# Four more value slots in the attention stage's page ring, and values two groups of pages later

## The reference

```python
kp = cache_k[i, page_table].reshape(db, past_len, MOBA_HEADS, HEAD_DIM)
vp = cache_v[i, page_table].reshape(db, past_len, MOBA_HEADS, HEAD_DIM)
...
k_mean = jnp.mean(kb.astype(jnp.float32), axis=3)
gate = jnp.einsum('bhtd,bhnd->bhtn', qh.astype(jnp.float32), k_mean)
_, sel = lax.top_k(gate, n_sel)        # the 3 best blocks of 256 tokens, and the own block
logits = q . k * scale - slope * distance, masked to the chosen blocks
p = softmax(logits);  out = p @ v
```

## Time and profile before

| | before |
|---|---|
| median of the runs | 1219.59 us (1218.74 to 1225.41) |
| profiled execution | 1221.69 us, its span 1220.0 us |
| PE busy | 1101.5 us, 90% of the span |
| DVE busy | 694.1 us, 57% |
| ACT busy | 562.6 us, 46% |
| POOL busy | 289.2 us, 24% |
| DMA | 182.58 MB, mean 150 GB/s |
| key page loads (kring) | 128 of 256 KB, median 3.7 us from issue to landing |
| value page loads (vring) | 128 of 256 KB, median 4.2 us from issue to landing |

### The profile page before, as it was taken

One profiled execution on the slowest core, in us unless ns is written; L12 is line 12 of the kernel. 1 busy time (PEld: TensorE's weight loads), 2 busy tenths in 40 slices (PEclk: granted clock), 3 DMA queues, 4 the chain that ended last, 5 costly groups with the idle time before them and its releaser, 6 DMA issues.

```text
span 1220.0 us, 20034 instructions
## 1 busy us (share of the span) xinstructions
PE 1101.5 (90%) x7015; PEld 990.8 (81%) x7015; DVE 694.1 (57%) x1191; ACT 562.6 (46%) x886; POOL 289.2 (24%) x274
## 2 busy tenths in 40 slices
PE   5999879976889999897999999988999699999995
PEld 3999768845555666566999999978999699999993
DVE  4753644454777777645666663445564666665333
ACT  3337501244666666645544443445333744543424
POOL 8400113320466667613100000213003300000101
PEclk9989958969899999988999999998999899999997
DMA  7334200064789889662444543443435244553411
GB/s 218 114 136 144 69 1 1 1 203 142 252 291 297 292 295 306 194 204 69 138 138 148 166 167 122 130 139 116 159 138 147 70 138 139 162 167 135 145 53 43
DMA packets 119121, 182.58 MB, mean 150 GB/s; under 512 B 6128, under 2 KB 59471, under 8 KB 118990
## 3 DMA queue, kind: packets, MB, share of 16 engines
q1 hardware_dynamic: 116274, 173.30, 43.2%
q0 software_dynamic: 2784, 8.47, 2.4%
HBM read 176.12 MB, written 5.63 MB: 149 GB/s over the span
## 4 chain that ended last, share of the span: by engine, by line
PE 73%; DVE 9%; ACT 7%; issue 3%; DMA 3%; POOL 2%; SPq 2%; DVEq 0%; ACTq 0%; POOLq 0%
PE bank L1652 68%; PE bank L1946 3%; DMA kring<-cache_k 2%; ACT hi L709 2%; POOL xl L652 1%; ACT xres L993 1%; DVE xres L1108 1%; DVE kTl L1108 1%; DVE lo L1101 1%; SPq L426 1%; POOL lo L625 1%; PE bank L1662 1%; ACT xh L709 1%; DMA xtok<-x_sample 1%; ACT kTh L709 0%
## 5 line engine op out<-in xcount | busy, mean ns | idle before, releaser
L1652 PE MATMUL bank<-xh,hi 128*128 128x320 f32 x1184 | 372.3, 314 | 33.5 <-POOL xl L652 26.1
L1652 PE MATMUL bank<-xl,hi 128*128 128x320 f32 x1184 | 370.1, 313 | 0.0
L1652 PE MATMUL bank<-xh,lo 128*128 128x320 f32 x1184 | 369.6, 312 | 0.0
L1101 DVE TENSOR_TENSOR lo<-raw,hi 128x2048 fp32r<-128x2048 f32 x102 | 242.2, 2375 | 188.6 <-ACT hi L709 188.6
L1652 PEld LDWEIGHTS bank<-xh,hi 128*128 128x128 f32 x1184 | 226.1, 191 | 36.2 <-issue 31.3
L709 ACT ACTIVATE hi<-raw 128x2048 fp32r (+1 forms) x102 | 194.8, 1910 | 107.6 <-PE bank L1652 107.6
L1652 PEld LDWEIGHTS bank<-xl,hi 128*128 128x128 f32 x1184 | 226.3, 191 | 0.1
L1652 PEld LDWEIGHTS bank<-xh,lo 128*128 128x128 f32 x1184 | 226.0, 191 | 0.0
L1108 DVE TENSOR_TENSOR kTl<-bank,kTh 128x512 fp32r<-128x512 f32 x128 | 88.0, 689 | 77.3 <-ACT kTh L709 75.8
L1652 PE MATMUL bank<-hh,hi 128*128 128x320 f32 x416 | 129.4, 311 | 1.3 <-DVE hraw L1108 1.3
L1652 PE MATMUL bank<-hh,lo 128*128 128x320 f32 x416 | 128.5, 309 | 0.0
(11 more groups left out here) (387 smaller groups left out, 1498.4 us busy)
## 6 DMA issues: line engine op xcount, KB each, us to landing
raw<-w_up SPq DMA_DIRECT2D x44, 1024.0 KB
kring<-cache_k SPq DMA_DIRECT2D x128, 256.0 KB, 3.7
vring<-cache_v SPq DMA_DIRECT2D x128, 256.0 KB, 4.2
raw<-w_down SPq DMA_DIRECT2D x8, 2048.0 KB
raw<-w_in_mix SPq DMA_DIRECT2D x7, 2048.0 KB
raw<-w_in_sc SPq DMA_DIRECT2D x8, 1024.0 KB
raw<-w_down SPq DMA_DIRECT2D x4, 1536.0 KB
raw<-w_out_mix SPq DMA_DIRECT2D x2, 2048.0 KB
```

Source lines behind the costliest of these rows:

```text
L1101: dve.tensor_tensor(lo[:, p], weight(n)[:, :, 256 * p:256 * p + 256], hi[:, p], ALU.subtract)\
L1652: return pe.matmul(out, lhsT, rhs, start=start, stop=stop, **kw)
```

## The change

The value pages get four more slots, in the half of `raw` that is idle during attention, so eight in all; the keys keep their two. The list of places is now the same for all readers (`kpages`, `vpages`, with `KS` = 2 and `VS` = 8). A value pair waits for POOL's work on the pair eight before it instead of four. Beside that, SP's step `n` issues pairs 2n - 12 and 2n - 11 instead of 2n - 10 and 2n - 9: values stand six groups behind keys instead of five. The units at which ACT, POOL and PE use the pairs are unchanged. The first value load also waits for the state's stores (7 stores), since the state lies in the same half of `raw`, and the load of slot `S_OUT + 1` into that half waits until all values are split. `load_list` of steps 0 and 1 moves ahead of two waits on PE and DVE.

```diff
-params_in xtok_in hist_in wba_in pt_in raw_in k_in0 k_in1 v_in0 v_in1 v_in2 v_in3 s0_in0 stores
+params_in xtok_in hist_in wba_in pt_in raw_in k_in0 k_in1 v_in0 v_in1 v_in2 v_in3 v_in4 v_in5 v_in6 v_in7 s0_in0 stores
...
+        spare_raw = raw[:, 0:4096].rearrange("p (j c) -> p j c", c=512)
+        kpages = [kring[:, 1], kring[:, 0]]
+        vpages = [vring[:, i] for i in range(4)] + [spare_raw[:, 2 * i:2 * i + 2] for i in range(4)]
+        KS, VS = len(kpages), len(vpages)
+        V_LAG = 12
...
-            for n in range(4 * NB + 5):
+            for n in range(4 * NB + V_LAG // 2):
+                if n < 4 * NB:
+                    load_list(n)
                 if n == 0:
                     PE.wait(sp_, "o1")
                     DV.wait(sp_, "qg2")
                 if n == 1:
                     PE.wait(sp_, "stS2")
                 if n < 4 * NB:
-                    load_list(n)
-                    after(sp_, "kT_mm", 4 * n - 4)
-                    x = (n + 1) % 2
-                    load_pair(kring[:, x, 0:2], a["cache_k"][0], f"k_in{x}", 2 * n)
-                    load_pair(kring[:, x, 2:4], a["cache_k"][0], f"k_in{x}", 2 * n + 1)
-                if n == 5:
+                    after(sp_, "kT_mm", 4 * (n - KS) + 4)
+                    k = kpages[n % KS]
+                    load_pair(k[:, 0:2], a["cache_k"][0], f"k_in{n % KS}", 2 * n)
+                    load_pair(k[:, 2:4], a["cache_k"][0], f"k_in{n % KS}", 2 * n + 1)
+                if n == V_LAG // 2:
                     PE.wait(sp_, "po1")
-                for m in (2 * n - 10, 2 * n - 9):
+                    sp_.wait_ge(s["stores"], 16 * 7)
+                for m in (2 * n - V_LAG, 2 * n - V_LAG + 1):
                     if m >= 0:
-                        after(sp_, "v_lo", m - 3)
-                        load_pair(vring[:, m % 4], a["cache_v"][0], f"v_in{m % 4}", m)
+                        after(sp_, "v_lo", m - VS + 1)
+                        load_pair(vpages[m % VS], a["cache_v"][0], f"v_in{m % VS}", m)
                         listed.pop(2 * m), listed.pop(2 * m + 1)
             sp_.wait_ge(s["stores"], 16 * 11)
+            sp_.wait_ge(s["v_lo"], VALL)
             slot_free(S_OUT + 1)
...
-                act.wait_ge(s[f"v_in{n % 4}"], 32 * (n // 4 + 1))
+                act.wait_ge(s[f"v_in{n % VS}"], 32 * (n // VS + 1))
...
-                copy(vhs[n % 3], vring[:, n % 4]).then_inc(s["v_hi"], 1)
+                copy(vhs[n % 3], vpages[n % VS]).then_inc(s["v_hi"], 1)
```

More of the change, by code:

```diff
@@ L624, in _ @@
                 pool.wait_ge(s["v_hi"], n + 1)
-                pool.tensor_tensor(vls[n % 3], vring[:, n % 4], vhs[n % 3], ALU.subtract).then_inc(s["v_lo"], 1)
+                pool.tensor_tensor(vls[n % 3], vpages[n % VS], vhs[n % 3], ALU.subtract).then_inc(s["v_lo"], 1)
                 b = n // VUNITS + 2
@@ L1466, in v_lo @@
                 dve.wait_ge(s["v_hi"], n + 1)
-                tt(vls[n % 3], vring[:, n % 4], vhs[n % 3], ALU.subtract).then_inc(s["v_lo"], 1)
+                tt(vls[n % 3], vpages[n % VS], vhs[n % 3], ALU.subtract).then_inc(s["v_lo"], 1)
             kT_lo(0)
@@ L1940, in transpose @@
                 g, h = divmod(n, H)
-                x = (g + 1) % 2
                 if h == 0:
-                    pe.wait_ge(s[f"k_in{x}"], 64 * (g // 2 + 1))
+                    pe.wait_ge(s[f"k_in{g % KS}"], 64 * (g // KS + 1))
                 after(pe, "kT_lo", n - 2)
                 for j in range(4):
-                    ins = pe.transpose(bank[n % 3][:, P * j:P * j + P], kring[:, x, j, P * h:P * h + P], ident[:, :])
+                    ins = pe.transpose(bank[n % 3][:, P * j:P * j + P], kpages[g % KS][:, j, P * h:P * h + P], ident[:, :])
                 ins.then_inc(s["kT_mm"], 1)
```

## The result

| | before | after |
|---|---|---|
| median of the runs | 1221.12 us (4 runs, 1218.74 to 1225.41) | 1233.83 us (4 runs, 1231.56 to 1238.18) |
| ratio, with its 95% interval | | 1.011 (1.0082 to 1.0138) |
| profiled execution, its span | 1221.69 us, 1220.0 us | 1232.57 us, 1230.8 us |
| key page loads, median to landing | 3.7 us | 3.6 us |
| value page loads, median to landing | 4.2 us | 4.9 us (`vring`), 4.8 us (`raw`) |

The change costs 12.7 us, 1.1%, where +5.4 was forecast; 1233.8 lies just outside the range of 1213 to 1233. The forecast was added to 1219.6 us, and the same kernel measured 1221.1 beside the changed one, so 1.5 us of the level are the base; what has to be explained is 12.7 against 5.4. The granted clock of TensorE was the same over the span (0.949 before, 0.950 after), and so is the work. What changed is what the engines wait for.

What follows compares the result with a forecast made beforehand. The attention stage was taken to hang on the order of waits, with DVE's run covering PE's key stalls. Pair 6's delays, 3 x 1.2 + 3 x 0.6 = +5.4 us, on 1219.6 gave 1225.0 us; range 1213 to 1233.

Steps and rivals of the forecast that it cites:

- The bound: Attention rounds: PE's work, then the DVE and ACT chain set the 28.4 us; key stalls lie in the chain's shadow.
- rival A: Attention: key stalls are on the path, so all 13.0 us of key waits come back, 1206.6 us; chance 0.13.
- One sign that the prediction named: PE's wait before a round's first value matmul was to grow from 1.0 to 2 us or more.
- Eight slots: Key loads: SP never waits for the subtraction, keys 21 go out 2.0 us sooner; gain at unit 2 none.
- rival B: Pairs land by E + 6.2, DVE's run is not pushed; 1.9 us come back at unit 14, 1217.7 us; chance 0.20.
- Pair 6 at unit 0: ACT waits 2.5 us for pair 6, pushing DVE's run 1.2 us in three rounds, 0.6 in three: +5.4 us.
- Pair 0, "hidden, by 0.4 us": ACT before the exponentials: pair 0 lets them start at 431.6, the DVE run pushes them to 431.96 anyway; no cost.
- Pairs 2 and 4, "none, up to 1 us a round": ACT at units 8 and 12: up to 2 us late, no cost, up to 1 us a round if landings are slower.
- Start, end and last weight load: Stage's ends: later first values cost nothing; last weight load between nothing and +1.9 us, taken as nothing.
- Rival C: Bursts overlap, each landing grows by 1 us: 1231.0 us, or 1232.9 with the last weight load late; chance 0.25.
- Slower: Whole kernel: a measured time above 1225.7 us, made up of C and the rest of the forecast's own case; chance 0.36.

Runs made afterwards that it cites:

- e1: Eight value slots with the old lag of five groups (V_LAG 10 instead of 12 in the changed kernel): 1218.85 us beside 1218.47, ratio 1.000.
- e9: Block sums and ranks, some 1.84 us of DVE's work per round, left out of the kernel with eight slots and the old lag: 1207.48 us beside 1219.36, 0.9893.
- e7: The changed kernel with pairs 6 and 7 of each sequence issued one group earlier, as before the change: 1230.88 us beside 1219.36, 1.0092.
- e12: The changed kernel with pairs 0, 1, 6 and 7 issued one step earlier, only pairs 2 to 5 late: 1225.09 us beside 1220.46, 1.0030.
- e3: The kernel before, with only the stage's last weight load held until all values are split: 1217.65 us beside 1218.47, 0.9999.
- e10: The changed kernel with the odd value pairs' loads left out, their readers taking the even pair's page: 1230.38 us beside 1220.46, 1.0070.
- e8: Block sums and ranks, some 1.84 us of DVE's work per round, left out of the kernel before: 1212.68 us beside 1219.36, 0.9934.
- e6: The changed kernel with pairs 0 and 1 of each sequence issued one group earlier, as before the change: 1231.9 us beside 1219.36, 1.0087.

## Why the prediction was wrong

**The bound.** Right. DVE's run covers the key stalls: e1 removes them for nothing, e9 shows that they are worth 5 us where the run is shorter. The faster rival A is out. One sign that the prediction named did not come: PE's wait before the first value matmul was to grow from 1.0 to 2 us or more. It is 1.03 us in the kernel after, and also in e1, where the keys come in time; so it was not the measure of PE's slack. What PE has over shows earlier in the round, where it waits for a unit's rest on DVE:

```profile
469.52 0.47 PE L1660 MATMUL bank<-kTh,qp 128*128 128x512 f32 x1 [0.78 <-DVE kTl L1116]
```

**Eight slots.** Right: no gain at unit 2, and 1.7 us in the trace of e1 at unit 14, where 1.9 had been worked out under rival B.

The loads hang on two points of a round: E, the end of unit 13's transposes, releases pair 6's burst, and the end of unit 1's transposes, which I call E1, releases pair 0's. In the round shown these are 451.40 and 458.60:

```profile
450.80 0.60 PE L1953 MATMUL bank<-ident,kring 128*128 128x128 f32 x4
...
458.00 0.60 PE L1953 MATMUL bank<-ident,kring 128*128 128x128 f32 x4
```

The six full rounds after, against what the prediction had:

| us | forecast | measured, mean (range) |
|---|---|---|
| pair 6 starts on ACT, from E | 7.4 | 7.76 (7.18 to 8.33) |
| unit 3's rest starts, from E | 9.1 | 9.33 (8.75 to 9.90) |
| shift ends, from E | 15.6 | 15.81 (15.23 to 16.38) |
| E1, from E | 6.17 | 7.03 (6.18 to 7.76) |
| pair 0 starts on ACT, from E1 | 7.4 | 8.10 (7.56 to 8.51) |
| exponentials start, from E | 15.6 | 16.58 (16.04 to 17.15) |

**Pair 6 at unit 0.** The mechanism was as described; a size was off. Unit 3's rest starts 1.58 us behind the start of pair 6's rounding in each of the six rounds, and the way from E to it grew by 6.8 us in the sum, where 5.4 had been worked out. (The +5.0 of the first table is another thing: it counts from the biases, which the late pairs 2 and 4 had moved already.) The term that was mis-sized is the 7.15 us from the first key issue to the pair, which took 7.58 for pair 6. Over the 18 pairs, the pair's second DMA left SP 2.71 us after the first key issue on the mean (2.45 forecast) and landed 5.00 us later (4.7).

**Pair 0, "hidden, by 0.4 us".** This step failed: +4.4 us. The cover of 0.4 is the difference of two paths, DVE's run behind pair 6 and ACT's copy of pair 0. A landing that is longer for both moves both and leaves the cover. What moved pair 0's path alone is its start: the text left E1 where it had been, 422.52 - 416.35 = 6.17 us behind E, and it came 7.03 behind E, in the round shown 7.20. And pair 0's landing took 0.3 us more than pair 6's (7.92 from the first key issue). So pair 0 let the exponentials start at E + 16.6, when the shift had been ready since E + 15.8. The margin was also smaller than the spread of the landings that I had read (4.4 to 5.5 in one burst), so "hidden" was not a value to take.

**Pairs 2 and 4, "none, up to 1 us a round".** This step failed as well, and it is what moved E1. Two units of slack between ACT and PE for the pair itself were counted, but not what is queued behind `v_hi` on ACT. With pair 4 at 452.71 two key copies and the queries' rounding wait behind it, DVE stands for 3.35 us, and unit 2's rest moves by 0.6 us:

```profile
454.29 1.30 DVE L1116 TENSOR_TENSOR kTl<-bank,kTh 128x512 fp32r<-128x512 f32 x2 [3.35 <-ACT kTh L717]
```

PE shows the same wait twice, before a product of unit 15 and one of unit 0, both ahead of unit 1's transposes:

```profile
455.13 0.41 PE L1660 MATMUL bank<-kTl,qp 128*64 128x512 f32 x1 [0.28 <-DVE kTl L1116]
...
456.50 0.49 PE L1660 MATMUL bank<-kTh,qp 128*128 128x512 f32 x1 [0.29 <-POOL qp L619]
```

In e1, where no pair is late, E1 comes 6.2 us behind E in every round; in e7, where pair 6 is early and pair 4 late, 6.4 to 7.3 us. So it is not pair 6 that moves it. The delay of the biases itself costs nothing here, since unit 3's rest waits for pair 6 anyway; it comes out in e12, where pair 6 is in time. In round 2 the late values reach into PE's own part: ACT waits 3.05 us for pair 2 (at 322.48), PE behind it for DVE's rests, and E comes 8.99 us after the first value matmul instead of 7.18.

It is the argument that the prediction made for pair 6, and did not make for pair 4. Together: the forecast was 5.4, the rounds grew by 12.9; of the 7.5 between them 4.4 are pair 0, 1.8 are E in round 2, and 1.4 (6.8 - 5.4) the later landing of pair 6, up to 0.1. This is read from one trace and from what e1, e7 and e12 change in it; a run with pairs 2 to 5 alone in time was not made.

**Start, end and last weight load.** Right: nothing (e3, and no difference behind the six rounds).

**The rivals.** Rival C had the direction: landings are later. Its price, 1 us for each of six landings, gave 1231.0. The landings grew by 0.6 on the mean, of which e10 puts 0.4 on the odd pairs' traffic; its reason, that a burst lies over the next, is not shown (see e10). The loss was larger all the same: C laid it on pair 6 alone, where pairs 4 and 0 pay too. B is out: pair 6 came 7.2 to 8.3 us behind E, and B needed 6.2. The rule of the Trainium skill (DMA: Bandwidth & Descriptors, on where the fixed cost goes in the anatomy of one DMA) gives, as an estimate, 5.6 us from the first key issue to the pair. The page fits it to single DMAs that GpSimd issues, and these are six that SP issues in a row. The kernel after took 7.0 to 8.3: the measurement decides.

**The chances.** Slower had 0.36 and C 0.25. The terms of pair 0 and of pair 4 had costs on one side only, none below nothing, and I added both at nothing; a sum of such terms lies at the lower end of what it can be. Nor are they independent: pair 4's delay moves the point from which pair 0's burst leaves.

What stays open: how the 5.0 us from the issue of a pair's second DMA to its landing divide between the queue and the transfer, and what pair 4 costs by itself.

## What to carry to other kernels

When a load is moved later in an in-order issue queue, work out for each consumer when it lands and what is queued behind that consumer's wait on its engine, not only who needs the data. A cover is the difference of two paths: ask what moves the start of each, and don't count on a margin smaller than the spread of the landings. More buffers remove a wait only where something else does not end at the same time, so take the cover away once (as e8 and e9 do) before paying for buffers. And where several late loads share a chain, undo them together as well as singly: a single one can show little, where the next one takes its place.

## What the runs showed of the hardware

I had expected that DMAs issued behind a load don't touch it, and that a landing is a fixed time with some scatter. In e6, with four more DMAs behind pair 6, it landed 0.7 us later on the mean of six (8.3 against 7.6). SP's timeline of its worst burst:

```profile
448.44 2.25 SPq L431 DMA_DIRECT2D kring<-cache_k  x4
450.80 1.88 SPq L431 DMA_DIRECT2D raw<-cache_v  x4
452.77 2.21 SPq L431 DMA_DIRECT2D vring<-cache_v  x4
```

Twelve DMAs of 256 KB leave within 6.5 us, 6.6 us behind the burst before (441.84), and the pair of the second row is there 9.9 us after the first key issue. But the count behind is not all: in e7 pair 4 has four more behind it as well and landed as in the kernel after (7.45 against 7.70 us, means of six). There the burst before had begun 8.7 to 10.6 us earlier (9.4 in one round, 431.68 to 441.12), not 6.6. That two bursts in flight are what makes the difference is my reading; no run isolates it, and with eight DMAs in a burst the kernel after shows no such difference (pair 4 at 8.3 to 9.8 us behind the burst before 7.70, pair 6 at mostly 6.6 us 7.58).
